# Layer one of a decoder trunk: VectorE turns three of a head's ten blocks of probabilities

## The chip, the cores and the metric

The kernel runs on one core of one Trainium2 chip. The metric is the device time of one execution in microseconds (us); less is better. All times below are of the kernel before the change.

## The reference, cut to what matters

The trunk has two layers over 512 tokens of width 1024, all in float32. Layer one is sparse attention: 16 heads of 128, one shared key and value, and for each query the 128 keys that an indexer has chosen. Layer two is a dilated window attention with 16 heads. Each layer ends in a gated output projection.

```python
s = jnp.einsum('bqhd,bqkd->bhqk', qb, k_sel).astype(jnp.float32)
s = jnp.where(valid[:, None], s, -jnp.inf)
p = jax.nn.softmax(s, axis=-1).astype(v.dtype)
return jnp.einsum('bhqk,bqkd->bqhd', p, v_sel)
...
return (o * jax.nn.silu(z)) @ w_out
```

The kernel does layer one's attention over all causal keys, with a bias that rules out those which were not chosen.

## The kernel before, in words

Every product of two float32 matrices is made of three matmuls: each operand is split into a high half (`_hi`, made by ScalarE) and a low half (`_lo`, what is left, made by GpSimd for weights and queries), and high by high, high by low and low by high are added in PSUM. The program of each engine is written out by hand, and semaphores join them. Each engine takes its instructions in the order written. The two layers' heads are numbered through: n = 0 to 15 in layer one, 16 to 31 in layer two.

The scores of a head are four row blocks of 128 queries; block i has i+1 blocks of 128 keys, so that there are ten blocks of 128 by 128. In layer one `head_a(hd)` is one step of a pipeline over the heads, on each engine:

- TensorE: the scores of head hd-2 (`scores`), half of the query projection of head hd (`project`, eight steps of three matmuls), the output of head hd-3 (`output`, for each block column j three matmuls, after a wait for the low half of that column), the other half of the projection, and then `turn_probs(hd - 2)`: the ten blocks of probabilities are turned with ten matmuls against the identity, into three PSUM banks (column 0 with four blocks, column 1 with three, columns 2 and 3 with three).
- VectorE: `mask_scores` (bias, negation and row maximum of the scores), `rope` of head hd-1's query (two products with the sine, one with the cosine, one sum), `invert` (the reciprocal of the four row sums), `gate` of head hd-3 (its output times the SiLU of the gate), `probs_lo` (the low halves of the turned probabilities, one instruction for each bank).
- ScalarE: the high half of a weight tile (`split_w`), `exps` (the four exponentials with their sums), the query's high half, `probs_hi` (the high halves of the turned probabilities, one for each bank).
- GpSimd: the low half of a weight tile (`split_w`), `normalise` (the four row blocks of probabilities times the inverse of their sums), the query's low half (`rope_lo`).

`head_a` runs for hd = 0 to 18, and heads 0 to 15 are attended in steps 2 to 17. In step 17 there is no rotation but a gate's scaling. After step 18 TensorE goes on to the output projection of layer one. Layer two turns nearly all its blocks on VectorE (`turn_blocks`): sixteen instructions, each of which turns the 32 by 32 parts of all ten blocks at one place (32 partitions, ten blocks of 32 elements).

Of the kernel before, what the change touches and what calls it, by code (L numbers as in the profile page):

```python
# [7 lines left out]
F32 = mybir.dt.float32  # L8
F32R = mybir.dt.float32r
ALU = mybir.AluOpType  # L10
ACT = mybir.ActivationFunctionType

P = 128
# [3 lines left out]
HEADS, HEAD_DIM = 16, 128  # L17
# [12 lines left out]
OFF = [P * i * (i + 1) // 2 for i in range(QB)]  # L30
COLS = P * QB * (QB + 1) // 2
T_OFF = [0, SEQ, SEQ + 3 * P, SEQ + 5 * P]
# [11 lines left out]
G_Q = [G_Z[-1] + 1] + list(range(G_Z[-1] + 3, G_Z[-1] + 2 + HEADS + LATE_GATES))  # L44
# [21 lines left out]
R_Q = R_K + 1  # L66
# [20 lines left out]
S_BANK, T_BANK = 2, 5  # L87
# [12 lines left out]
CUT = T_OFF[2]  # L100
# [3 lines left out]
def turned_before(n):  # L104

    by_vector = sum(x in VECTOR_HEADS for x in range(n))
    return n - by_vector, by_vector
# [7 lines left out]
def build(nc, xT, x_rows, gains, weights, rope_tables, dilated_bias, causal_bias, ident_in, outT, out_rows):  # L115
    with ExitStack() as ctx:
# [3 lines left out]
        def sem(name):  # L120
            return ctx.enter_context(nc.semaphore(name))

        ps = ctx.enter_context(nc.psum_tensor("ps", [P, 8, SEQ], F32))
# [35 lines left out]
        probs = sb("probs", [P, COLS])  # L159
# [3 lines left out]
        pT_hi = sb("pT_hi", [P, COLS], F32R)  # L163
        pT_lo = sb("pT_lo", [P, COLS], F32R)
# [12 lines left out]
        score = sb("score", [P, COLS - P])  # L177
        left = neg_s[:, 0:COLS - P]

        turned = bias_a  # L180

        ordered = neg_s
# [15 lines left out]
        inv_den = sb("inv_den", [P, QB])  # L198
# [38 lines left out]
            sem("scores_done"), sem("scores_read"), sem("exp_done"), sem("inv_ready"), sem("probs_ready"))  # L237
        blocks_turned, turned_hi_ready, turned_lo_ready = (
            sem("blocks_turned"), sem("turned_hi_ready"), sem("turned_lo_ready"))
        probs_turned, pT_hi_ready, pT_lo_ready, o_done, gated_ready = (  # L240
            sem("probs_turned"), sem("pT_hi_ready"), sem("pT_lo_ready"), sem("o_done"), sem("gated_ready"))
        o_lo_ready, o_hi_ready, y_done, residual_ready = (
# [88 lines left out]
        def _(pe):  # L331
# [141 lines left out]
            def turn_probs(n):  # L473
                pe.wait_ge(probs_ready, n * QB + QB)
                if n:
                    pe.wait_ge(gated_ready, n)
                for b, js in enumerate(((0,), (1,), (2, 3))):
                    for j in js:
                        for i in range(j, QB):
                            at = T_OFF[j] - T_OFF[js[0]] + (i - j) * P  # L480
                            src = OFF[i] + j * P
                            last = pe.transpose(ps[:, T_BANK + b, at:at + P], probs[:, src:src + P], ident[:, :])  # L482
                    last.then_inc(probs_turned, 1)
# [18 lines left out]

            def output(n, high, low):
                for j in range(QB):
                    pe.wait_ge(pT_lo_ready, turned_before(n)[0] * 3 + min(j, 2) + 1)
                    out = ps[:, T_BANK, j * P:SEQ]
                    vs, cols = slice(j * P, (j + 1) * P), slice(T_OFF[j], T_OFF[j] + SEQ - j * P)
                    pe.matmul(out, high[:, vs], pT_hi[:, cols], start=(j == 0), stop=False)
                    pe.matmul(out, high[:, vs], pT_lo[:, cols], start=False, stop=False)  # L509
                    last = pe.matmul(out, low[:, vs], pT_hi[:, cols], start=False, stop=(j == QB - 1))  # L510
                last.then_inc(o_done, 1)
# [209 lines left out]
        def _(act):  # L721
# [109 lines left out]
            def exps(n):  # L831
                by_tensor, by_vector = turned_before(n)
                if by_vector:

                    act.wait_ge(probs_ready, n * QB)
                elif by_tensor:
                    act.wait_ge(probs_turned, by_tensor * 3)
                for i in range(QB):
                    act.wait_ge(scores_read, n * QB + i + 1)
                    cols = slice(OFF[i], OFF[i] + (i + 1) * P)  # L840
                    act.activation(probs[:, cols], neg_s[:, cols], ACT.Exp, bias=neg_max[:, i:i + 1], scale=-1.0,  # L841
                                   accum_out=den[:, i:i + 1]).then_inc(exp_done, 1)

            def probs_hi(n):
                for b, (at, end) in enumerate(((0, T_OFF[1]), (T_OFF[1], T_OFF[2]), (T_OFF[2], COLS))):
                    act.wait_ge(probs_turned, turned_before(n)[0] * 3 + b + 1)
                    act.activation(pT_hi[:, at:end], ps[:, T_BANK + b, 0:end - at],  # L847
                                   ACT.Copy).then_inc(pT_hi_ready, 1)

            def turned_hi(n):  # L850
                act.wait_ge(blocks_turned, turned_before(n)[1] + 1)
# [159 lines left out]
        def _(dve):  # L1011
# [121 lines left out]
                dve.tensor_tensor(rotated[:, R_K % 2, :], by_cos[:, :], by_sin[:, :],  # L1133
                                  ALU.add).then_inc(rotated_ready, 1)

            def rope(r, g):
                n, half = n_of(g), P // 2

                past = r - R_IQ - 1 - (r > R_K) - (r > R_B)
                dve.wait_ge(tile_done, g + 1)  # L1140
                dve.wait_ge(*rotated_at(r - 1))
                for out, other in ((slice(0, half), slice(half, P)), (slice(half, P), slice(0, half))):
                    dve.tensor_tensor(by_sin[out, :], ps[other, BANK[n], :], scaled[other, 1, :],  # L1143
                                      ALU.mult).then_inc(sin_ready, 1)

                dve.wait_ge(sin_ready, 2 * past + 2)
                dve.tensor_tensor(ps[:, BANK[n], :], ps[:, BANK[n], :], scaled[:, 0, :], ALU.mult).then_inc(cos_ready, 1)
                dve.wait_ge(cos_ready, past + 1)
                dve.wait_ge(rope_lo_ready, r - 1)
                dve.tensor_tensor(rotated[:, r % 2, :], ps[:, BANK[n], :], by_sin[:, :],  # L1150
                                  ALU.add).then_inc(bank_read[BANK[n]], 1)
# [80 lines left out]
            def turn_blocks(n):  # L1232
# [9 lines left out]
                                             source[rows_at:rows_at + 32, :, cols_at:cols_at + 32])  # L1242
                last.then_inc(blocks_turned, 1)

            def probs_lo(n):
                for b, (at, end) in enumerate(((0, T_OFF[1]), (T_OFF[1], T_OFF[2]), (T_OFF[2], COLS))):
                    dve.wait_ge(pT_hi_ready, turned_before(n)[0] * 3 + b + 1)
                    dve.tensor_tensor(pT_lo[:, at:end], ps[:, T_BANK + b, 0:end - at],  # L1248
                                      pT_hi[:, at:end].bitcast(F32), ALU.subtract).then_inc(pT_lo_ready, 1)
# [31 lines left out]
            def head_a(hd):  # L1281
                attend, roped, finish = 2 <= hd < HEADS + 2, 1 <= hd < HEADS + 1, 3 <= hd < HEADS + 3
                if attend:
                    mask_scores(hd - 2, bias_a, lambda i: OFF[i])
                if roped:
                    rope(R_Q + hd - 1, G_Q[hd - 1])
                if attend:
                    invert(hd - 2)
                if hd > HEADS:
                    z = hd - LATE_GATES - 1  # L1290
                    scale_gate(z, G_Z[z])
                if finish:
                    gate(hd - 3, hd - 3)
                if attend:
                    probs_lo(hd - 2)

            def head_b(hd):
# [164 lines left out]
        def _(pool):  # L1462
# [42 lines left out]
            def normalise(n):  # L1505
                pool.wait_ge(inv_ready, n + 1)
                for i in (3, 2, 1, 0):
                    cols = slice(OFF[i], OFF[i] + (i + 1) * P)
                    pool.tensor_scalar(probs[:, cols], probs[:, cols], inv_den[:, i:i + 1], 1.0, ALU.mult,  # L1509
                                       ALU.mult).then_inc(probs_ready, 1)  # L1510

            def order(n):

                pool.wait_ge(inv_ready, n + 1)
                blocks = ordered[:, :].rearrange("p (b c) -> p b c", c=P)
                for i in (3, 2, 1, 0):
                    for first, count, place, step in GROUPS[i]:
                        cols = slice(OFF[i] + first * P, OFF[i] + (first + count) * P)
                        last = pool.tensor_scalar(blocks[:, place:place + (count - 1) * step + 1:step, :],  # L1519
                                                  probs[:, cols].rearrange("p (b c) -> p b c", c=P),  # L1520
                                                  inv_den[:, i:i + 1], 1.0, ALU.mult, ALU.mult)
                    last.then_inc(probs_ready, 1)

            def turned_lo(n):
                number = turned_before(n)[1]
                pool.wait_ge(o_done, n)
                for k, part in enumerate((slice(0, CUT), slice(CUT, COLS))):
                    pool.wait_ge(turned_hi_ready, 2 * number + k + 1)
                    pool.tensor_tensor(pT_lo[:, part], turned[:, part], pT_hi[:, part].bitcast(F32),  # L1529
                                       ALU.subtract).then_inc(turned_lo_ready, 1)  # L1530

            def head_a(hd):
                attend, rope = 2 <= hd < HEADS + 2, 1 <= hd < HEADS + 1
                if 0 < hd < HEADS + LATE_GATES:
                    split_w(G_Q[hd] + 2)
                if attend:
                    normalise(hd - 2)
                if rope:
                    slot = (hd - 1) % 2
                    rope_lo(R_Q + hd - 1, q_hi[:, slot, :], q_lo[:, slot, :])  # L1540
# [135 lines left out]
```

## Time and profile before

| what | value |
| --- | --- |
| median of 3 runs | 932.15 us (931.74 to 933.51) |
| the profiled execution | 931.12 us |
| its span in the profile | 929.3 us |
| busy share of the span: TensorE matmuls, VectorE, ScalarE, GpSimd | 99%, 65%, 46%, 59% |

The span is the part of the execution that the profiler saw; 1.8 us of the execution lie around it. A busy share is the mean over the whole span, in which stages with different limits follow on one another: the attention of layer one runs from about 163 to 329 us.

### The profile page before, as it was taken

The numbers are of one execution on the slowest core, as the hardware profiler recorded it, in microseconds if no ns is written. First come the engines' busy times: TensorE is split into PE (matmuls) and PEld (weight loads), VectorE is DVE, ScalarE is ACT, GpSimd is POOL, SyncE is SP. The second block draws the span as 40 slices with busy tenths as digits, with TensorE's granted clock in tenths as the row PEclk, the third lists the DMA queues.
The fourth block names the chain that finished last, engine by engine and source line by source line (L and its number), as shares of the span: only waits on it lengthen the run. The fifth ranks groups of instructions, "written<-read, shape, count | busy, mean of one in ns | idle before, by whom it ended". The sixth has DMA issues, their size and how long they took to land.

```text
span 929.3 us, 13299 instructions
## 1 busy us (share of the span) xinstructions
PE 920.9 (99%) x4865; PEld 801.1 (86%) x4865; DVE 600.5 (65%) x1283; ACT 426.5 (46%) x776; POOL 551.7 (59%) x419
## 2 busy tenths in 40 slices
PE   9999999999999999999999999999999999999997
PEld 8898888788888888889898898989898888988887
DVE  7898898676677541145776666667767666665234
ACT  6765333454455542253443535452443435453334
POOL 2776545555555544457666677666766667774544
PEclk9999999999999999999999999999999999999999
DMA  8322322112111122222222222222222222132412
GB/s 335 134 92 82 123 91 91 46 46 68 46 46 47 67 84 98 95 88 69 70 90 92 91 80 65 83 92 89 71 70 90 91 91 81 56 114 69 129 53 91
DMA packets 24689, 81.48 MB, mean 88 GB/s; under 512 B 2864, under 2 KB 4144, under 8 KB 24624
## 3 DMA queue, kind: packets, MB, share of 16 engines
q1 hardware_dynamic: 23472, 79.06, 25.7%
q10 hardware_dynamic: 1152, 1.57, 0.5%
q8 instruction: 39, 0.64, 0.3%
q14 instruction: 26, 0.21, 0.1%
HBM read 78.52 MB, written 2.10 MB: 87 GB/s over the span
## 4 chain that ended last, share of the span: by engine, by line
PE 95%; DVE 2%; POOL 1%; issue 0%; DMA 0%; ACT 0%; DVEq 0%; SPq 0%; POOLq 0%
PE ps L384 17%; PE ps L385 17%; PE ps L386 17%; PE ps L518 6%; PE ps L519 6%; PE ps L520 6%; PE ps L419 3%; PE ps L418 3%; PE ps L417 3%; PE ps L482 2%; PE ps L469 2%; PE ps L470 2%; PE ps L471 2%; PE ps L509 1%; PE ps L510 1%; PE ps L499 1%
## 5 line engine op out<-in xcount | busy, mean ns | idle before, releaser
L1468 POOL TENSOR_TENSOR w_lo<-w_raw,w_hi 128x1024 fp32r<-128x1024 f32 x136 | 329.4, 2429 | 175.0 <-ACT w_hi L726 174.3
L384 PE MATMUL ps<-u_hi,w_hi 128*128 128x512 f32 (+1 forms) x712 | 275.5, 387 | 0.3 <-POOL w_lo L1468 0.2
L385 PE MATMUL ps<-u_lo,w_hi 128*128 128x512 f32 (+1 forms) x712 | 274.5, 386 | 0.0
L386 PE MATMUL ps<-u_hi,w_lo 128*128 128x512 f32 (+1 forms) x712 | 274.5, 385 | 0.0
L384 PEld LDWEIGHTS ps<-u_hi,w_hi 128*128 128x128 f32 x712 | 133.7, 188 | 26.4 <-DVE u_lo L1057 0.6
L386 PEld LDWEIGHTS ps<-u_hi,w_lo 128*128 128x128 f32 x712 | 133.7, 188 | 25.8
L385 PEld LDWEIGHTS ps<-u_lo,w_hi 128*128 128x128 f32 x712 | 133.7, 188 | 25.3
L726 ACT ACTIVATE w_hi<-w_raw 128x1024 fp32r<-128x1024 f32 x136 | 141.7, 1053 | 25.7 <-DMA w_raw<-weights 16.4
L1241 DVE STREAM_TRANSPOSE bias_a<-neg_s 32x320 f32<-32x320 f32 x240 | 120.6, 503 | 25.1 <-POOL neg_s L1519 22.1
L841 ACT ACTIVATE probs<-neg_s,neg_max 128x128 f32<-128x128 f32 (+3 forms) x128 | 70.5, 552 | 51.9 <-DVE neg_max L1223 51.8
L1529 POOL TENSOR_TENSOR pT_lo<-bias_a,pT_hi 128x896 fp32r<-128x896 f32 (+1 forms) x30 | 46.6, 1574 | 70.4 <-ACT pT_hi L855 70.4
L855 ACT ACTIVATE pT_hi<-bias_a 128x896 fp32r<-128x896 f32 (+1 forms) x30 | 20.5, 731 | 126.9 <-DVE bias_a L1241 126.9
L419 PE MATMUL ps<-w_hi,u_lo 128*128 128x256 f32 x256 | 72.4, 283 | 0.0
L418 PE MATMUL ps<-w_lo,u_hi 128*128 128x256 f32 x256 | 72.4, 283 | 0.0
L417 PE MATMUL ps<-w_hi,u_hi 128*128 128x256 f32 x256 | 72.4, 283 | 0.0
L1519 POOL TENSOR_SCALAR neg_s<-probs,inv_den 128x256 f32<-128x256 f32 x90 | 38.9, 453 | 54.0 <-DVE inv_den L1230 54.0
L1143 DVE TENSOR_TENSOR by_sin<-ps,scaled 64x512 f32<-64x512 f32 x94 | 64.7, 689 | 4.7 <-PE ps L386 0.7
L1248 DVE TENSOR_TENSOR pT_lo<-ps,pT_hi 128x384 fp32r<-128x384 f32 (+1 forms) x51 | 27.5, 596 | 53.9 <-ACT pT_hi L847 53.9
L1509 POOL TENSOR_SCALAR probs<-probs,inv_den 128x512 f32<-128x512 f32 (+1 forms) x68 | 35.4, 541 | 39.7 <-DVE inv_den L1230 39.7
L518 PE MATMUL ps<-o_hi,w_hi 128*128 128x512 f32 (+1 forms) x136 | 51.6, 379 | 0.0
L519 PE MATMUL ps<-o_lo,w_hi 128*128 128x512 f32 (+1 forms) x136 | 51.2, 377 | 0.0
L520 PE MATMUL ps<-o_hi,w_lo 128*128 128x512 f32 (+1 forms) x136 | 51.2, 377 | 0.0
(206 smaller groups left out, 1729.3 us busy)
## 6 DMA issues: line engine op xcount, KB each, us to landing
w_raw<-weights SPq DMA_DIRECT2D x136, 512.0 KB, 3.3
gated<-x_rows SPq DMA_DIRECT2D x4, 512.0 KB, 8.0
h<-x_turned SPq DMA_DIRECT2D x7, 256.0 KB, 5.6
w_raw<-weights SPq DMA_DIRECT2D x4, 256.0 KB, 4.7
table<-rope_tables SPq DMA_DIRECT2D x2, 512.0 KB, 7.2
neg_s<-weights SPq DMA_DIRECT2D x1, 512.0 KB, 6.8
outT<-h ACTq DMA_DIRECT2D x4, 128.0 KB, 1.7
outT<-h SPq DMA_DIRECT2D x4, 128.0 KB, 1.9
```

The costliest lines, as they stand in the source:

```text
L384: pe.matmul(out, w_hi[:, g % SLOTS, blk], u_hi[:, k, tokens], start=(at == 0), stop=False)
L385: pe.matmul(out, w_hi[:, g % SLOTS, blk], u_lo[:, k, tokens], start=False, stop=False)
L386: last = pe.matmul(out, w_lo[:, g % SLOTS, blk], u_hi[:, k, tokens], start=False, stop=(at == KT - 1))
L417: pe.matmul(out, u_hi[:, k, tokens], high, start=(j % 2 == 0 and at == 0), stop=False)
L418: pe.matmul(out, u_hi[:, k, tokens], low, start=False, stop=False)
L419: last = pe.matmul(out, u_lo[:, k, tokens], high, start=False, stop=(j % 2 == 1 and at == KT - 1))
L518: pe.matmul(out, w_hi[:, g % SLOTS, blk], hi[:, tokens], start=first, stop=False)
L519: pe.matmul(out, w_hi[:, g % SLOTS, blk], lo[:, tokens], start=False, stop=False)
L520: return pe.matmul(out, w_lo[:, g % SLOTS, blk], hi[:, tokens], start=False, stop=final)
L726: act.activation(w_hi[:, g % SLOTS, :], w_raw[:, g % 2, :], ACT.Copy).then_inc(w_hi_ready, 1)
L1241: last = dve.transpose(target[cols_at:cols_at + 32, :, rows_at:rows_at + 32], source[rows_at:rows_at + 32, :, cols_at:cols_at + 32])
L1468: pool.tensor_tensor(w_lo[:, g % SLOTS, :], w_raw[:, g % 2, :], w_hi[:, g % SLOTS, :].bitcast(F32), ALU.subtract).then_inc(w_lo_ready, 1)
```

## The change

For the heads of layer one alone:

- TensorE turns seven blocks (columns 0 and 1) and no longer the last three (column 2's two and column 3's one).
- GpSimd (`normalise_apart` in place of `normalise`) writes these three blocks, normalised, to the space `apart` first, and then the other seven in place: six instructions in place of four.
- VectorE turns the three blocks from `apart` to `apart_turned` in sixteen instructions (`turn_apart`, 32 partitions and three blocks of 32 elements each), after `gate` and ahead of `probs_lo`, which makes two low halves in place of three.
- ScalarE makes the high half of the third part from `apart_turned` in place of a PSUM bank, and so waits for VectorE there.
- GpSimd makes the third part's low half (`apart_lo`), as the first instruction of the next step.
- TensorE's `output` waits for that low half ahead of column 2.
- VectorE's `invert` moves from behind the rotation to between the rotation's two products with the sine and the one with the cosine.

```diff
+        apart, apart_turned = score[:, 0:3 * P], score[:, 3 * P:6 * P]
...
-                for b, js in enumerate(((0,), (1,), (2, 3))):
+                for b, js in enumerate(((0,), (1,)) if n < HEADS else ((0,), (1,), (2, 3))):
...
-                    pe.wait_ge(pT_lo_ready, turned_before(n)[0] * 3 + min(j, 2) + 1)
+                    if n < HEADS and j == 2:
+                        pe.wait_ge(apart_lo_ready, n + 1)
+                    elif j < 3:
+                        pe.wait_ge(pT_lo_ready, 2 * turned_before(n)[0] + j + 1)
...
+                    if n < HEADS and b == 2:
+                        act.wait_ge(apart_done, n + 1)
+                        source = apart_turned
+                    else:
+                        act.wait_ge(probs_turned, 2 * turned_before(n)[0] + b + 1)
+                        source = ps[:, T_BANK + b, 0:end - at]
+                    act.activation(pT_hi[:, at:end], source, ACT.Copy).then_inc(pT_hi_ready, 1)
...
+                if inverted is not None:
+                    invert(inverted)
...
+            def turn_apart(n):
+                dve.wait_ge(apart_ready, n + 1)
+                if n:
+
+                    dve.wait_ge(pT_hi_ready, 3 * n)
+                    dve.wait_ge(apart_lo_ready, n)
+                source, target = (t.rearrange("p (b c) -> p b c", c=P) for t in (apart, apart_turned))
+                for rows_at in range(0, P, 32):
+                    for cols_at in range(0, P, 32):
+                        last = dve.transpose(target[cols_at:cols_at + 32, :, rows_at:rows_at + 32],
+                                             source[rows_at:rows_at + 32, :, cols_at:cols_at + 32])
+                last.then_inc(apart_done, 1)
...
                 if roped:
-                    rope(R_Q + hd - 1, G_Q[hd - 1])
-                if attend:
+                    rope(R_Q + hd - 1, G_Q[hd - 1], hd - 2 if attend else None)
+                elif attend:
                     invert(hd - 2)
...
                 if attend:
+                    turn_apart(hd - 2)
                     probs_lo(hd - 2)
...
+            def normalise_apart(n):
+
+                pool.wait_ge(inv_ready, n + 1)
+                if n:
+                    pool.wait_ge(apart_done, n)
+                for i, at in ((3, P), (2, 0)):
+                    cols = slice(OFF[i] + 2 * P, OFF[i] + (i + 1) * P)
+                    last = pool.tensor_scalar(apart[:, at:at + (i - 1) * P], probs[:, cols], inv_den[:, i:i + 1], 1.0,
+                                              ALU.mult, ALU.mult)
+                last.then_inc(apart_ready, 1)
+                for i in (3, 2, 1, 0):
+                    cols = slice(OFF[i], OFF[i] + min(i + 1, 2) * P)
+                    pool.tensor_scalar(probs[:, cols], probs[:, cols], inv_den[:, i:i + 1], 1.0, ALU.mult,
+                                       ALU.mult).then_inc(probs_ready, 1)
...
+            def apart_lo(n):
+                pool.wait_ge(pT_hi_ready, 3 * n + 3)
+                pool.tensor_tensor(pT_lo[:, CUT:COLS], apart_turned, pT_hi[:, CUT:COLS].bitcast(F32),
+                                   ALU.subtract).then_inc(apart_lo_ready, 1)
...
+                if hd >= 3:
+                    apart_lo(hd - 3)
                 if 0 < hd < HEADS + LATE_GATES:
                     split_w(G_Q[hd] + 2)
                 if attend:
-                    normalise(hd - 2)
+                    normalise_apart(hd - 2)
```

On VectorE, a step of layer one from the rotation to the next head's scores stands in this order in the kernel before (out<-in, partitions by elements):

```order
L1143 TENSOR_TENSOR by_sin<-ps,scaled 64x512 x2
L1147 TENSOR_TENSOR ps<-ps,scaled 128x512
L1150 TENSOR_TENSOR rotated<-ps,by_sin 128x512
L1230 RECIPROCAL inv_den<-den 128x4
L1273 TENSOR_TENSOR gated<-ps,gated 128x512
L1248 TENSOR_TENSOR pT_lo<-ps,pT_hi 128x512
L1248 TENSOR_TENSOR pT_lo<-ps,pT_hi 128x384 x2
L1220 TENSOR_TENSOR neg_s<-ps,bias_a 128x128
```

In the changed kernel the same place, after the two products with the sine and the moved reciprocal, reads:

```order
L1161 TENSOR_TENSOR ps<-ps,scaled 128x512
L1164 TENSOR_TENSOR rotated<-ps,by_sin 128x512
L1302 TENSOR_TENSOR gated<-ps,gated 128x512
L1268 STREAM_TRANSPOSE score<-score 32x3x32 x16
L1277 TENSOR_TENSOR pT_lo<-ps,pT_hi 128x512
L1277 TENSOR_TENSOR pT_lo<-ps,pT_hi 128x384
L1234 TENSOR_TENSOR neg_s<-ps,bias_a 128x128
```

Sixteen turning instructions have come between `gate` and the low halves, one low half of 384 columns has gone, and the next head's scores stand behind all of them.

On GpSimd, a step in the kernel before, from the weight tile's low half on:

```order
L1468 TENSOR_TENSOR w_lo<-w_raw,w_hi 128x1024
L1509 TENSOR_SCALAR probs<-probs,inv_den 128x512
L1509 TENSOR_SCALAR probs<-probs,inv_den 128x384
L1509 TENSOR_SCALAR probs<-probs,inv_den 128x256
L1509 TENSOR_SCALAR probs<-probs,inv_den 128x128
L1492 TENSOR_TENSOR q_lo<-rotated,q_hi 128x512
```

And in the changed kernel:

```order
L1550 TENSOR_SCALAR score<-probs,inv_den 128x256
L1550 TENSOR_SCALAR score<-probs,inv_den 128x128
L1555 TENSOR_SCALAR probs<-probs,inv_den 128x256 x3
L1555 TENSOR_SCALAR probs<-probs,inv_den 128x128
L1523 TENSOR_TENSOR q_lo<-rotated,q_hi 128x512
L1580 TENSOR_TENSOR pT_lo<-score,pT_hi 128x384
L1499 TENSOR_TENSOR w_lo<-w_raw,w_hi 128x1024
```

The normalising has six instructions, the three blocks for VectorE first, and the third part's low half stands between the query's low half and the next weight tile's.

## Rows read from the trace of the kernel before

**Rows 1.** The page's first part: busy time, share of the span, instructions.

```profile
PE 920.9 (99%) x4865; PEld 801.1 (86%) x4865; DVE 600.5 (65%) x1283; ACT 426.5 (46%) x776; POOL 551.7 (59%) x419
```

**Rows 2.** Busy time by engine in one step's window: PE, PEld, DVE, ACT, POOL, granted clock.

```profile
239.41:249.72 10.31, 10.31 (x59) 9.03 (x57) 7.00 (x19) 5.26 (x15) 5.71 (x6) 1.00 0.15 53
```

**Rows 3.** Timeline of VectorE, one step: start, us, what, idle before.

```profile
308.65 0.28 DVE L1220 TENSOR_TENSOR neg_s<-ps,bias_a 128x128 f32<-128x128 f32 x1
...
310.74 1.41 DVE L1143 TENSOR_TENSOR by_sin<-ps,scaled 64x512 f32<-64x512 f32 x2
...
313.52 0.17 DVE L1230 RECIPROCAL inv_den<-den 128x4 f32<-128x4 f32 x1
313.60 0.66 DVE L1273 TENSOR_TENSOR gated<-ps,gated 128x512 f32<-128x512 f32 x1
317.42 1.62 DVE L1248 TENSOR_TENSOR pT_lo<-ps,pT_hi 128x512 fp32r<-128x512 f32 x3 [3.16 <-ACT pT_hi L847]
318.96 0.28 DVE L1220 TENSOR_TENSOR neg_s<-ps,bias_a 128x128 f32<-128x128 f32 x1
```

**Rows 4.** Timeline of TensorE: the turning, and what comes next.

```profile
316.16 1.25 PE L482 MATMUL ps<-ident,probs 128*128 128x128 f32 x10
317.17 0.36 PE L462 MATMUL ps<-k_both,q_hi 128*128 128x256 f32 x1
```

**Rows 5.** Layer two's turning on VectorE: its line's view, then its timeline.

```profile
L1241 DVE STREAM_TRANSPOSE bias_a<-neg_s x240: 498/503/509, 447.5 to 817.8; 32x320 f32<-32x320 f32 x120
499.18 1.53 DVE L1241 STREAM_TRANSPOSE bias_a<-neg_s 32x320 f32<-32x320 f32 x3 [0.47 <-POOL neg_s L1519]
```

**Rows 6.** VectorE by line and shape, 180 to 290 us: busy us, mean ns, idle before.

```profile
L1223 DVE CUSTOM_DVE_ANT_0 neg_s<-ps,bias_a 128x512 f32<-128x512 f32 x11 | 7.5, 686 | 0.0
...
L1223 DVE CUSTOM_DVE_ANT_0 neg_s<-ps,bias_a 128x256 f32<-128x256 f32 x11 | 4.6, 421 | 0.0
...
L1220 DVE TENSOR_TENSOR neg_s<-ps,bias_a 128x128 f32<-128x128 f32 x11 | 3.1, 282 | 0.0
L1230 DVE RECIPROCAL inv_den<-den 128x4 f32<-128x4 f32 x10 | 1.7, 169 | 0.0
```

**Rows 7.** GpSimd by line and shape, 445 to 810 us.

```profile
L1519 POOL TENSOR_SCALAR neg_s<-probs,inv_den 128x256 f32<-128x256 f32 x60 | 28.0, 478 | 54.0 <-DVE inv_den L1230 54.0
...
L1529 POOL TENSOR_TENSOR pT_lo<-bias_a,pT_hi 128x384 fp32r<-128x384 f32 x14 | 14.3, 1023 | 0.0
L1519 POOL TENSOR_SCALAR neg_s<-probs,inv_den 128x128 f32<-128x128 f32 x30 | 12.1, 403 | 0.0
```

**Rows 8.** Timelines of ScalarE and GpSimd in a step, and of GpSimd in layer two.

```profile
310.86 0.71 ACT L841 ACTIVATE probs<-neg_s,neg_max 128x512 f32<-128x512 f32 x1
315.81 1.28 POOL L1492 TENSOR_TENSOR q_lo<-rotated,q_hi 128x512 fp32r<-128x512 f32 x1
319.18 2.42 POOL L1468 TENSOR_TENSOR w_lo<-w_raw,w_hi 128x1024 fp32r<-128x1024 f32 x1 [2.09 <-ACT w_hi L726]
...
499.11 4.75 POOL L1468 TENSOR_TENSOR w_lo<-w_raw,w_hi 128x1024 fp32r<-128x1024 f32 x2
```

**Rows 9.** Timeline of VectorE, the first attended head.

```profile
168.43 0.17 DVE L1230 RECIPROCAL inv_den<-den 128x4 f32<-128x4 f32 x1
173.25 1.62 DVE L1248 TENSOR_TENSOR pT_lo<-ps,pT_hi 128x512 fp32r<-128x512 f32 x3 [4.66 <-ACT pT_hi L847]
174.78 0.28 DVE L1220 TENSOR_TENSOR neg_s<-ps,bias_a 128x128 f32<-128x128 f32 x1
```

**Rows 10.** Timelines of VectorE, ScalarE and TensorE, the last attended head.

```profile
324.01 0.69 DVE L1273 TENSOR_TENSOR gated<-ps,gated 128x512 f32<-128x512 f32 x1 [1.24 <-ACT gated L829]
325.72 1.36 ACT L847 ACTIVATE pT_hi<-ps 128x512 fp32r<-128x512 f32 x3 [1.81 <-PE ps L482]
327.57 0.39 PE L508 MATMUL ps<-pT_hi,v_hi 128*128 128x512 f32 x1
...
328.77 0.29 PE L508 MATMUL ps<-pT_hi,v_hi 128*128 128x256 f32 x1
```

More of the change, by code:

```diff
@@ L239, in build @@
             sem("blocks_turned"), sem("turned_hi_ready"), sem("turned_lo_ready"))
+        apart_ready, apart_done, apart_lo_ready = sem("apart_ready"), sem("apart_done"), sem("apart_lo_ready")
         probs_turned, pT_hi_ready, pT_lo_ready, o_done, gated_ready = (
@@ L836, in exps @@
                 elif by_tensor:
-                    act.wait_ge(probs_turned, by_tensor * 3)
+                    act.wait_ge(probs_turned, 2 * by_tensor)
                 for i in range(QB):
@@ L845, in probs_hi @@
                 for b, (at, end) in enumerate(((0, T_OFF[1]), (T_OFF[1], T_OFF[2]), (T_OFF[2], COLS))):
-                    act.wait_ge(probs_turned, turned_before(n)[0] * 3 + b + 1)
-                    act.activation(pT_hi[:, at:end], ps[:, T_BANK + b, 0:end - at],
-                                   ACT.Copy).then_inc(pT_hi_ready, 1)
+                    if n < HEADS and b == 2:
[5 more added lines that the diff above has]
+                    act.activation(pT_hi[:, at:end], source, ACT.Copy).then_inc(pT_hi_ready, 1)
             def turned_hi(n):
@@ L1134, in key_rope, with rope @@
                                   ALU.add).then_inc(rotated_ready, 1)
-            def rope(r, g):
+            def rope(r, g, inverted=None):
                 n, half = n_of(g), P // 2
@@ L1243, in turn_blocks @@
                 last.then_inc(blocks_turned, 1)
+            def turn_apart(n):
[9 more added lines that the diff above has]
+                last.then_inc(apart_done, 1)
             def probs_lo(n):
-                for b, (at, end) in enumerate(((0, T_OFF[1]), (T_OFF[1], T_OFF[2]), (T_OFF[2], COLS))):
+                parts = ((0, T_OFF[1]), (T_OFF[1], T_OFF[2]), (T_OFF[2], COLS))
+                for b, (at, end) in enumerate(parts[0:2] if n < HEADS else parts):
                     dve.wait_ge(pT_hi_ready, turned_before(n)[0] * 3 + b + 1)
```

## The prediction

> **What bounds the kernel now.** The page comes first: TensorE has matmuls in flight for 99% of the span, and the busiest other engine, VectorE, works for 65% of it [rows 1]. The busy time in the window of one step of layer one then shows this stage's own limit: TensorE is busy for all of its 10.31 us, at the full granted clock (1.00), VectorE for 7.00 and GpSimd for 5.71 [rows 2]. So a step lasts as long as TensorE's work in it, and what the others have to spare is room. VectorE's timeline shows how large the room is and where it lies: from one head's first mask instruction (308.65) to the next one's (318.96) pass 10.31 us, and the only large gap is the 3.16 us ahead of the low halves [rows 3]. All else on VectorE takes 10.31 - 3.16 = 7.15 us.
>
> **What TensorE saves.** The ten turns take 317.17 - 316.16 = 1.01 us until the next matmul starts, 0.101 each [rows 4]. Three fewer give 0.30 us for a head and 4.85 us for 16 heads. TensorE would then need 10.01 us for a step. That is all the change can give, and VectorE has to keep up with 10.01 for it.
>
> **What VectorE takes on.** No instruction of the trace turns 96 elements, so the price of the sixteen has to be bounded. The same operation with 320 elements takes 503 ns, and three of them in a row take 1.53 us, so that one starts (1.53 - 0.503) / 2 = 0.514 us after the other: 11 ns more than it lasts, with no overlap [rows 5]. How it scales is the question on which all depends:
> - In proportion to the elements it would be 0.3 of 0.514, 0.154 us. I exclude this: a reciprocal of four elements alone lasts 169 ns [rows 6].
> - With that instruction as floor, and the 11 ns: 0.18 us. This is the lower bound.
> - VectorE's other work grows by (686 - 421) / 256 = 1.035 ns an element [rows 6]. Taken off the 503 ns for 224 fewer elements, 271 ns are left, with the 11 ns 0.282 us. This is nearest in kind, and I take it.
> - The nearest row in size, 128 columns in 282 ns [rows 6], less 32 elements at that slope and with the 11 ns gives 0.26 us.
> - With no gain from the smaller size: 0.514 us, the upper bound.
>
> Call this pitch p. The sixteen take 16p - 0.01 us. Out of VectorE's step goes the third low half: three take 1.54 us from 317.42 to 318.96 [rows 3], and of the 384 wide one I take 0.46. Two new waits on other engines, ahead of the turning and behind it, cost about 0.03 each. The moved reciprocal costs the same in its new place. VectorE's step becomes 7.15 - 0.46 + 0.06 - 0.01 + 16p = 6.74 + 16p. At p = 0.282 that is **11.25 us**, more than TensorE's 10.01 and more than the 10.31 of before: VectorE becomes the bound and a head costs 0.94 us more. TensorE's step is shorter than VectorE's from p = 0.204 on, and above p = 0.223 the change loses in every step.
>
> The Trainium skill speaks to this price ("VectorE: DVE Perf Modes"). Its section on the TRN2 errata has VectorE's SBUF instructions cost 58 cycles and one for each element at 0.96 GHz, by which 320 elements would take 394 ns. The trace has 503 for them, so it does not agree. By the rule a turn of 96 would be 160 ns, and an estimate by it is a step of 9.3 us on VectorE, so that TensorE would stay the bound. The section on the three transpose paths gives 311 ns for VectorE on 128 by 128 in bf16; no run here shows that one, and as an estimate it would put 96 elements near 0.28 us.
>
> **Do the others fit into 11.25 us?** I follow one step from T, the end of the sixteen turns.
> - ScalarE's third high half: three take 1.36 us [rows 10], so about 0.5, done at T+0.5; GpSimd's third low half 1.02 us [rows 7], done at T+1.6; the weight tile's low half 2.42 [rows 8], done at T+4.1.
> - VectorE makes its two low halves (1.1) and starts the mask at T+1.1. From the mask's start the two products with the sine end after 312.15 - 308.65 = 3.5 us [rows 3], and the last exponential is done earlier, after 2.9 [rows 8]. So the inverse comes at T+4.7, when GpSimd is free.
> - GpSimd's six instructions cost four times 0.478 and two times 0.403 [rows 7], 2.7 us: `apart` is ready at T+5.6, all probabilities at T+7.5, the query's low half at T+8.8 (1.28 more).
> - VectorE has ended `gate` at T+1.1 + 5.6 = T+6.7 (314.26 - 308.65 before [rows 3]), later than `apart` is ready. This is what the moved inverse does: in its old place, 1.3 us later, VectorE would stand for some 0.2 us here.
> - TensorE turns seven blocks at T+7.5, begins the scores at T+8.8 and has them done by T+10.7; VectorE masks them at T+12.4. Its output's wait for the third low half (T+12.9 in the next round) comes behind half a projection and is over before it is reached (T+13.4).
>
> So nothing makes the step longer than VectorE's own work. TensorE loses 11.25 - 10.01 = 1.2 us a step, ahead of the turning (for GpSimd's probabilities) and ahead of the scores (for the query's low half).
>
> **The sum.** Head 0 has more room, since TensorE's step is longer there: VectorE ends the rotation about 168.6, the turns 173.1, two low halves 174.3, against 174.78 before [rows 9]: -0.5 us. The next fourteen masks follow 11.25 apart in place of 10.31: +13.2. The last attended head has no rotation, so here TensorE's wait is the limit. From its mask's start M (318.96 before), `gate` ends at M+5.7 (324.70 [rows 10]), the turns at M+10.3, the first low half at M+11.0, the second at M+11.5, GpSimd's third at M+11.9. Output column 0 starts at M+11.0 and column 2 1.2 us later at M+12.2, in place of 328.77 = M+9.8 [rows 10]: +2.4. Behind it TensorE has the output projection and layer two, in which it works without a gap of note [rows 1], so the delay stays. Sum: -0.5 + 13.2 + 2.4 = **+15.1 us**. On the profiled execution's 931.12 this gives 946.2, and since that lies 1.03 under the median of 932.15, the median comes to 947.3; I say 947.
>
> **The rivals.**
> - *VectorE becomes the bound* (my forecast). For it: the 503 ns and the slope in its own engine's rows. At p = 0.26 (step 10.90) the sum is -0.8 + 8.3 + 2.1 = 9.6, at p = 0.30 (step 11.54) -0.2 + 17.2 + 2.7 = 19.7: 941 to 953. 0.80.
> - *TensorE stays the bound; faster.* It needs p below 0.204, a fixed part near the reciprocal's 169 ns and little else, or a fixed part that the next instruction hides as it does between the mask's instructions. Against it: the turns of 320 do not overlap at all [rows 5]. The gain is 4.85 less up to 1 us at the last head: 928. This is where the skill's 58 cycles would lead. 0.11. At p from 0.204 to 0.223 the two effects cancel and the time is within 0.2%: 0.03.
> - *VectorE waits as well.* If GpSimd is slower while VectorE turns (against it: beside layer two's turning, from 499.18 on, two weight tiles' low halves take 4.75 us, as fast as layer one's 2.42 each [rows 5, 8]), or if the inverse reaches it late, the turning starts late: 0.5 us a step give 15 x 0.5 = 7.5 more, 954 to 955. 0.06 together with the upper bound p = 0.514, whose step of 15.0 us would give about 1,000.
>
> **How the numbers follow.** The likeliest case and the lower part of the last give slower with 0.86; faster 0.11; same 0.03. A change under 0.2% (1.9 us) could not be told from none. The likeliest case holds 941 to 953 with 0.80 less its own tails. To hold 8 in 10 the range takes in a pitch down to about 0.24 (a step of 10.6, +5 us) and half of the waiting case: 936 to 955.
>
> **What would show it.** Right: in the changed profile VectorE is busy for 95% or more of a step of layer one, the step is about 11.2 us between masks, a turn takes near 270 ns, TensorE has gaps of some 0.7 and 0.5 us ahead of the turning and of the scores, and layer two's steps are as before. Wrong: a turn of under 0.2 us with steps of 10.0; or turns as priced, but a longer step with idle time on VectorE ahead of the turning. The weakest number is the turn's fixed part, since sixteen of it lie in each step: 10 ns in it move the result by 2.4 us.

## The result and the profile after

The changed kernel takes 947.49 us (median of 6 runs, 946.59 to 947.93), the kernel before 932.50 (6 runs on the same chip): a ratio of 1.016, with a 95% interval of 1.0147 to 1.0173. The forecast was 947, slower, with a range of 936 to 955.

The page of the changed kernel, its first part (to be held against [rows 1]):

```profile
PE 924.5 (98%) x4817; PEld 796.2 (84%) x4817; DVE 663.0 (70%) x1523; ACT 428.5 (45%) x776; POOL 575.0 (61%) x467
```

TensorE has 48 instructions fewer, VectorE 240 more and 62 us more of work. The averages show no bound on VectorE, since 70% is far from full. The step does. Two steps of layer one in windows that reach from one head's first mask instruction to the next one's (to be held against [rows 2]):

```profile
309.22:320.35 11.13, 10.44 (x55) 8.64 (x54) 10.74 (x34) 5.39 (x14) 7.16 (x10) 1.00 0.16 48
320.35:331.49 11.14, 10.45 (x55) 8.64 (x54) 10.75 (x35) 5.40 (x14) 7.17 (x10) 1.00 0.15 49
```

The window is 11.13 us where it was 10.31. TensorE's busy time no longer fills it, and VectorE's 10.74 does but for the small gaps between its instructions. VectorE's timeline of that step (to be held against [rows 3]):

```profile
309.22 0.28 DVE L1234 TENSOR_TENSOR neg_s<-ps,bias_a 128x128 f32<-128x128 f32 x1
...
311.30 1.41 DVE L1155 TENSOR_TENSOR by_sin<-ps,scaled 64x512 f32<-64x512 f32 x2
312.74 0.18 DVE L1244 RECIPROCAL inv_den<-den 128x4 f32<-128x4 f32 x1
312.83 0.67 DVE L1161 TENSOR_TENSOR ps<-ps,scaled 128x512 f32<-128x512 f32 x1
313.54 0.69 DVE L1164 TENSOR_TENSOR rotated<-ps,by_sin 128x512 f32<-128x512 f32 x1
314.15 0.68 DVE L1302 TENSOR_TENSOR gated<-ps,gated 128x512 f32<-128x512 f32 x1
314.75 4.50 DVE L1268 STREAM_TRANSPOSE score<-score 32x96 f32<-32x96 f32 x16
319.28 1.16 DVE L1277 TENSOR_TENSOR pT_lo<-ps,pT_hi 128x512 fp32r<-128x512 f32 x2
320.35 0.28 DVE L1234 TENSOR_TENSOR neg_s<-ps,bias_a 128x128 f32<-128x128 f32 x1
```

No row has an idle time behind it in brackets: the 3.16 us ahead of the low halves are gone. The turning takes 4.50 us in one piece. The waits are now on TensorE, in the timeline of the same step (to be held against [rows 4]):

```profile
315.60 0.98 PE L487 MATMUL ps<-ident,probs 128*128 128x128 f32 x7 [0.44 <-POOL probs L1555]
316.84 0.39 PE L466 MATMUL ps<-k_both,q_hi 128*128 128x256 f32 x1 [0.25 <-POOL q_lo L1523]
```

They stand at the two places named beforehand, ahead of the turning (for the normalised probabilities) and ahead of the scores (for the query's low half). The brackets count from the end of the matmul before. By the starts, the turning comes 0.60 us and the scores 0.56 us later than they would right behind the matmuls before them, where 0.7 and 0.5 were forecast. Together that is what TensorE loses in a step: 11.13 us, against 9.96 in a kernel in which it doesn't wait (half of the turns, below). The chain that ended last shows VectorE's part over the whole program; before, 95% of it lay on TensorE and 2% on VectorE:

```profile
PE 76%; DVE 17%; issue 3%; DMA 2%; ACT 1%; POOL 1%; SPq 0%; DVEq 0%; ACTq 0%; POOLq 0%
```

**Where the time went.** The mask instructions of the heads are marks that both traces have. From mask 0 to the end of the span it is 765.75 us before (163.55 to 929.3) and 780.87 after (164.83 to 945.7): 15.12 more.

| stretch | before | after | difference | forecast |
| --- | --- | --- | --- | --- |
| mask 0 to mask 1 | 11.23 | 10.77 | -0.46 | -0.5 |
| mask 1 to mask 15 | 144.18 | 155.89 | +11.71 | +13.2 |
| mask 15 to layer two's first mask | 122.65 | 126.51 | +3.86 | +2.4 |
| from there to the end | 487.69 | 487.70 | +0.01 | 0 |

Mask 0 itself stands 1.28 us later after (164.83 for 163.55), ahead of all that was changed. In the other profiles of this study it stands at 164.35 or later, so this is taken for a difference between executions; the medians lie 15.0 us apart.

### The profile page after: what moved, and what is told of

The parts are those of the page before. It is cut to its first block, busy times and chain, and to the rows that moved or that the text cites. A ratio compares the mean times of both kernels' runs of the same rounds, so it can differ in the third digit from the quotient of the medians.

```text
span 945.7 us, 13521 instructions
## 1 busy us (share of the span) xinstructions
PE 924.5 (98%) x4817; PEld 796.2 (84%) x4817; DVE 663.0 (70%) x1523; ACT 428.5 (45%) x776; POOL 575.0 (61%) x467
## 4 chain that ended last, share of the span: by engine, by line
PE 76%; DVE 17%; issue 3%; DMA 2%; ACT 1%; POOL 1%; SPq 0%; DVEq 0%; ACTq 0%; POOLq 0%
PE ps L388 13%; PE ps L389 13%; PE ps L390 13%; DVE score L1268 6%; PE ps L526 6%; PE ps L528 6%; PE ps L527 6%; PE ps L423 3%; PE ps L422 3%; PE ps L421 3%; DVE by_sin L1155 2%; DVE pT_lo L1277 2%; DMA gated<-x_rows 1%; DVE u_lo L1069 1%; DVE neg_s L1237 1%
## 5 line engine op out<-in xcount | busy, mean ns | idle before, releaser
L1268 DVE STREAM_TRANSPOSE score<-score 32x96 f32<-32x96 f32 x256 | 68.8, 269 | 3.2
L1302 DVE TENSOR_TENSOR gated<-ps,gated 128x512 f32<-128x512 f32 x32 | 22.0, 686 | 44.1 <-PE ps L505 39.7
```

The lines of the kernel that those rows point to most:

```text
L1268: last = dve.transpose(target[cols_at:cols_at + 32, :, rows_at:rows_at + 32], source[rows_at:rows_at + 32, :, cols_at:cols_at + 32])
```

## The experiments

Theory A in all of them: VectorE's own queue, with sixteen turns of nearly fixed price, sets the step of the changed kernel. Its rivals are named with each. The first four ran on one chip, beside 932.03 us for the kernel before; the next four on a second, beside 932.31; the last two on a third, beside 932.07. Each ratio is to the kernel before on the same chip. A difference between two other kernels can be one between chips, on which the kernel before differs by up to 0.5 us.

**Half of the turns.** Is it VectorE's length, or the longer chain through ScalarE and GpSimd?

```diff
+                if n == 0:
+                    dve.memset(target[:, :, P // 2:P], 0.0)
-                for rows_at in range(0, P, 32):
+                for rows_at in range(0, P // 2, 32):
```

> The changed kernel with eight of the sixteen turning instructions left out (half of the rows of the three blocks are not turned, a zero stands there), all waits kept. Theory A (the length of VectorE's queue is the bound, sixteen times 0.282 us of it the turning): VectorE's step falls to 11.13 - 8 x 0.282 = 8.9 us, TensorE is the bound again with its three turns saved: steps of 10.0 us and 927.5 to 928.5 us in all, under the kernel before. Theory B (the longer chain through ScalarE and GpSimd is the bound, and VectorE only happens to be busy): steps stay over 10.3 us, 932 us or more.

Measured: 926.75 us (4 runs, 926.71 to 926.87), ratio 0.994 (0.9924 to 0.9957). The window of one step:

```profile
244.40:254.36 9.96, 9.96 (x56) 8.68 (x54) 8.67 (x26) 5.28 (x14) 7.21 (x10) 1.00 0.15 53
```

TensorE fills it again, and VectorE needs 8.67. All waits and the whole detour over ScalarE and GpSimd are still there; only eight instructions of a head are gone. So the detour costs nothing by itself, and TensorE's saving is real as soon as VectorE has the room. It is a little larger than forecast, as TensorE's timeline of this kernel shows:

```profile
252.02 0.93 PE L487 MATMUL ps<-ident,probs 128*128 128x128 f32 x7
252.70 0.36 PE L466 MATMUL ps<-k_both,q_hi 128*128 128x256 f32 x1
```

Seven turns take 0.68 us until the next matmul, where ten took 1.01 [rows 4]: 0.33 saved, not 0.30. The result lies 0.75 us under the expected range. Two causes can be seen: this 0.03 us in each step, and the interval from mask 1 to mask 2, which is 8.87 us where the kernel before has 10.10 (the moved inverse, see below).

**Narrower turns.** Is the price of a turn fixed, or does it go with the elements? The third block of each turn is left out:

```diff
-                        last = dve.transpose(target[cols_at:cols_at + 32, :, rows_at:rows_at + 32],
-                                             source[rows_at:rows_at + 32, :, cols_at:cols_at + 32])
+                        last = dve.transpose(target[cols_at:cols_at + 32, 0:2, rows_at:rows_at + 32],
+                                             source[rows_at:rows_at + 32, 0:2, cols_at:cols_at + 32])
```

> The changed kernel with each of the sixteen turning instructions over two of the three blocks (64 elements; the third block is not turned). Theory A (a large fixed part, 1.04 ns an element on top): an instruction every 0.249 us, 0.53 us less a step, steps of 10.6 us, 939 to 940 us in all. Theory B (the price goes with the elements): an instruction every 0.188 us, VectorE's step 9.6 us, TensorE the bound at 10.0, 930 us or less.

Measured: 938.24 us (4 runs, 937.83 to 940.12), ratio 1.0067 (1.0052 to 1.0082): theory A, though 0.8 us under the expected range. VectorE's timeline:

```profile
244.49 3.96 DVE L1268 STREAM_TRANSPOSE score<-score 32x64 f32<-32x64 f32 x16
248.48 1.16 DVE L1277 TENSOR_TENSOR pT_lo<-ps,pT_hi 128x512 fp32r<-128x512 f32 x2
249.56 0.28 DVE L1234 TENSOR_TENSOR neg_s<-ps,bias_a 128x128 f32<-128x128 f32 x1
...
260.16 0.28 DVE L1234 TENSOR_TENSOR neg_s<-ps,bias_a 128x128 f32<-128x128 f32 x1
```

A third less to turn takes the sixteen from 4.50 to 3.96 us, and the step to 260.16 - 249.56 = 10.60, as expected. What is missing to 939 lies in the last head: from mask 15 to the end of the span it is 612.6 us here and 614.2 in the changed kernel (see the last head by TensorE). Together with the line's view of this kernel and of the changed one the price is known at three widths, the third from [rows 5]:

```profile
L1268 DVE STREAM_TRANSPOSE score<-score x256: 222/236/243, 169.5 to 333.2; 32x64 f32<-32x64 f32 x128
```

```profile
L1268 DVE STREAM_TRANSPOSE score<-score x256: 253/269/276, 169.8 to 341.4; 32x96 f32<-32x96 f32 x128
```

From 64 to 96 elements it is 33 ns for 32, from 96 to 320 it is 234 ns for 224: 1.03 and 1.04 ns an element, on a fixed part of some 169 ns.

**The inverse back in its old place.**

```diff
-                    rope(R_Q + hd - 1, G_Q[hd - 1], hd - 2 if attend else None)
-                elif attend:
+                    rope(R_Q + hd - 1, G_Q[hd - 1])
+                if attend:
                     invert(hd - 2)
```

> The changed kernel with the inverse of the sums back behind the rotation. Theory A (VectorE's own queue sets the step, and the moved inverse keeps it free of waits): the inverse comes 1.3 us later, the three blocks apart are ready about 0.4 us after the gate ends, so each of 14 to 15 turnings starts 0.4 to 0.5 us later: 953 to 955 us, with that wait on GpSimd seen ahead of the turning. Theory B (GpSimd is ready early enough in either place): 947.5 us, no wait.

Measured: 954.87 us (4 runs, 953.64 to 955.23), ratio 1.0239 (1.0224 to 1.0254): theory A, 7.4 us more than the changed kernel. Its masks lie 11.62 us apart in place of 11.13. In its timeline VectorE waits once in each step:

```profile
250.68 0.66 DVE L1302 TENSOR_TENSOR gated<-ps,gated 128x512 f32<-128x512 f32 x1
251.72 4.52 DVE L1268 STREAM_TRANSPOSE score<-score 32x96 f32<-32x96 f32 x16 [0.39 <-POOL score L1550]
```

From the gate's start to the turning's it is 1.04 us in place of 0.60. So the moved inverse is what keeps GpSimd's three blocks ahead of VectorE.

**The last head by TensorE.** What does the end of layer one cost? The change is bound to a set of heads, here 0 to 14, and each counter of the semaphores is counted over that set:

```diff
+APART = range(HEADS - 1)
...
-                for b, js in enumerate(((0,), (1,)) if n < HEADS else ((0,), (1,), (2, 3))):
+                for b, js in enumerate(((0,), (1,)) if n in APART else ((0,), (1,), (2, 3))):
```

> The changed kernel, but the last head of layer one (head 15) has all ten blocks turned by TensorE as before. Theory A (the end of layer one costs 3.7 us of the loss, of which about 1.5 us are matmuls at half the clock after TensorE's wait of 2.7 us): 943.4 us, no wait over 1 us ahead of the last output and no matmuls at half clock there. Theory B (the end costs the 2.4 us that I had priced and the rest lies elsewhere): 945 us.

Measured: 943.40 us (4 runs, 943.09 to 944.47), ratio 1.012 (1.0105 to 1.0136): theory A; 4.1 us lie in the last head. The traces say so too, by what follows mask 15: 614.2 us in the changed kernel, 610.2 here. What they are made of shows in TensorE's timeline of the changed kernel at that place (to be held against [rows 10]):

```profile
337.38 0.98 PE L487 MATMUL ps<-ident,probs 128*128 128x128 f32 x7 [1.31 <-POOL probs L1555]
...
342.42 0.79 PE L516 MATMUL ps<-pT_hi,v_hi 128*128 128x512 f32 x1 [2.67 <-DVE pT_lo L1277]
343.01 0.63 PE L517 MATMUL ps<-pT_lo,v_hi 128*128 128x512 f32 x1
...
344.82 0.41 PE L516 MATMUL ps<-pT_hi,v_hi 128*128 128x256 f32 x1
...
345.80 0.44 PE L526 MATMUL ps<-o_hi,w_hi 128*128 128x512 f32 x1
```

and in two windows of it:

```profile
342.40:345.80 3.40, 3.38 (x13) 3.10 (x13) 2.04 (x3) 1.65 (x4) 0.89 (x1) 0.53 0.00 0
345.80:356.00 10.20, 10.20 (x47) 8.46 (x47) 7.08 (x5) 4.34 (x6) 5.14 (x3) 1.00 0.15 51
```

TensorE waits 1.31 us, turns, works a little and waits 2.67 us for the low halves (a wait that the kernel before doesn't have). Then a matmul of 512 columns lasts 0.63 us in place of 0.39, and the granted clock of the stretch is 0.53: nearly all of it at the lower level of 1.2 GHz. Head 15's output takes 345.80 - 342.42 = 3.38 us; head 14's, at the full clock, took 1.85 (332.63 to 334.48). That is 1.5 us, and in the stretch behind the clock is back at 1.00. In the kernel of this experiment TensorE waits once there, 1.28 us ahead of the turning (for the gate), and its matmuls of 512 columns stay at 0.39. The kernel with narrower turns waits 0.79 and then 2.11 us at this place; its granted clock stays at 1.00, and from the start of head 15's output to the output projection it takes 2.2 us in place of 3.4. This is why it came out under its range.

**The inverse alone, on the kernel before.**

```diff
+                if inverted is not None:
+                    invert(inverted)
...
-                    rope(R_Q + hd - 1, G_Q[hd - 1])
-                if attend:
+                    rope(R_Q + hd - 1, G_Q[hd - 1], hd - 2 if attend else None)
+                elif attend:
                     invert(hd - 2)
```

> The kernel before with one part of the change alone: the inverse of the sums between the sine and the cosine products. Theory A (TensorE is the bound of a step and never waits for GpSimd there): no difference, 931.5 to 932.5 us; GpSimd's normalising starts 1.2 us earlier in a step, unused. Theory B (the inverse's place is worth something by itself): faster by 0.2% or more.

Measured: 930.52 us (11 runs, 929.60 to 930.96), ratio 0.9979 (0.9970 to 0.9988). Here I was wrong: it is faster by 1.8 us, 0.21% with an interval of 0.12% to 0.30%, which is theory B's side. The timeline of TensorE in the kernel before and then in this one, at the turning of head 1, has the cause:

```profile
182.03 1.31 PE L482 MATMUL ps<-ident,probs 128*128 128x128 f32 x10 [1.64 <-POOL probs L1509]
```

```profile
181.50 1.31 PE L482 MATMUL ps<-ident,probs 128*128 128x128 f32 x10 [0.31 <-POOL probs L1511]
```

Three of the eight steps of the query projection that belongs into this step of the pipeline were already done in the step before, so TensorE's step is short there and it does wait for GpSimd, 1.64 us before and 0.31 now. From mask 0 to mask 15 it is 153.94 us in place of 155.41; where the other 0.3 us of the 1.8 lie is not shown. This wait comes once, and I had looked at windows of later heads.

**Every other head.** A turning head leaves VectorE 11.13 - 10.01 = 1.1 us behind TensorE. Does a head without it make up for that? The heads that turn are 0, 2, ... 14.

```diff
+APART = range(0, HEADS - 1, 2)
```

> The changed kernel with the change in heads 0, 2, 4, ... 14 alone; the other heads have all ten blocks turned by TensorE. Theory A (a turning step leaves VectorE 1.1 us behind TensorE; the moved inverse gives GpSimd 1.2 us of room, so that the next head's query and probabilities are still in time, and VectorE catches up in that step): no waits on TensorE, each of the 8 heads saves its 0.30 us, 2.4 us in all: 929.2 to 930.2 us, faster than the kernel before. Theory B (TensorE waits in each step in which VectorE is late): 932 us or more.

Measured: 929.37 us (6 runs, 928.95 to 930.53), ratio 0.9968 (0.9957 to 0.9980): faster than the kernel before. The windows of a turning head and of the next one:

```profile
285.52:296.66 11.14, 11.14 (x61) 9.65 (x60) 10.74 (x34) 5.12 (x14) 6.69 (x9) 1.00 0.15 49
296.66:305.77 9.11, 9.11 (x53) 8.05 (x53) 6.99 (x20) 5.51 (x14) 6.24 (x7) 1.00 0.19 58
```

The masks are 11.14 and 9.11 us apart, 20.25 for two heads where 20.60 were needed, and TensorE is busy in all of it: VectorE is late for one head and on time for the next.

The time is in the expected range, but not all by the expected way. That range took 2.4 us for the turns alone, and "no waits". The moved inverse is in this kernel too, and alone it gave 930.52 us on the same chip. So the turning by itself is worth 1.15 us by the medians, and the ranges of the two kernels overlap. In the traces it shows: from mask 0 to mask 15 it is 152.38 us, and 153.94 with the inverse alone. Two waits of TensorE are left, 0.17 us at head 1's turning and 0.78 at head 15's.

**Two of three heads.**

```diff
+APART = [n for n in range(HEADS - 1) if n % 3 < 2]
```

> As the kernel with every other head, but with the change in heads 0, 1, 3, 4, 6, 7, ... 13 (ten heads). Theory A (the room is between 1.1 and 1.5 us, and two turning steps in a row put VectorE 2.2 us behind): about 0.8 us of waits in each group of three heads, against 0.6 saved: 932 to 934 us. Theory B (the room holds two in a row): ten heads save 3.0 us, 929 us.

Measured: 933.66 us (10 runs, 932.71 to 934.72), ratio 1.0014 (1.0005 to 1.0023): theory A. A group takes 11.31 + 11.13 + 8.77 = 31.21 us between masks, where three heads at TensorE's pace would take 30.3: 0.9 us lost in each group, 0.8 expected.

**Every other head, inverse back.** The set of every other head with the diff of the inverse's old place.

> As the kernel with every other head, with the inverse back behind the rotation. Theory A (the moved inverse is what gives the room): a turning step is late by 1.5 us, the room is 0.3 us or none, so about 1.4 us of waits for each pair of heads: 936 to 941 us. Theory B (the room lies elsewhere): 930 us, as with the inverse moved.

Measured: 941.68 us (4 runs, 940.22 to 941.76), ratio 1.0094 (1.0081 to 1.0108). The way is theory A's, and the size is 0.7 us beyond its range: 12.3 us more than with the inverse moved. The masks place it. From mask 4 on a pair of heads takes 21.73 us, 1.48 more than the 20.25 with the inverse moved (1.4 expected). The first two pairs take 2.9 and 1.7 more. There TensorE waits 2.35 us at head 1's turning, and its ten turns behind that take 2.39 us in place of 1.31, at a granted clock of 0.63 and then 0.52, which the expectation didn't have.

**Without head 14, and every other head again.** The larger of the two waits that are left with every other head stands in TensorE's timeline at head 15's turning:

```profile
322.79 1.28 PE L500 MATMUL ps<-ident,probs 128*128 128x128 f32 x10 [0.78 <-DVE gated L1316]
```

```diff
-APART = range(0, HEADS - 1, 2)
+APART = range(0, HEADS - 2, 2)
```

> As the kernel with every other head, but head 14 is left to TensorE: the change in heads 0, 2, ... 12 alone. In the trace of the kernel with every other head TensorE waits 0.78 us for a gate ahead of head 15's turning, since VectorE is late from head 14. Theory A (that wait comes from head 14's turning): it is gone, at the price of one saving of 0.30 us: 0.5 us faster than with head 14, 928.9 us, which the times alone can hardly show and the trace can. Theory B (the wait belongs to the end of the layer as such): 0.3 us slower, 929.7 us, with the wait still there.

> The kernel with every other head once more, beside the one without head 14: 929.4 us, with the 0.78 us wait ahead of head 15's turning, and about 3 us faster than the kernel before.

Measured: 928.77 us (6 runs, 928.33 to 930.20; ratio 0.9966, 0.9954 to 0.9978) without head 14, 929.66 (7 runs, 929.05 to 930.20; ratio 0.9974, 0.9963 to 0.9985) with it. TensorE's waits in layer one are 0.8 us for the gate and 0.2 for probabilities in the second, and there is none in the first, so theory A holds by the trace; the times overlap and don't tell the two apart. The version with seven heads is the fastest of those that still compute the reference, 3.3 us under the kernel before. Of these, 1.8 are the moved inverse's. The seven heads' turning adds 1.5 by the medians (on another chip) and 2.4 by the spans of the profiled executions (926.3 us, and 928.7 with the inverse alone), which is seven times the 0.33 us of a head. Part of the difference lies outside the span, where the kernel with seven heads has 2.3 us in place of 1.8; the cause of that is open.

## Why the prediction was right, point by point

- **TensorE saves 0.30 us a head and VectorE has to keep up.** Right in kind; with half the turns the step is 9.96 us and the whole 926.75. The saving is 0.33: the forecast took a tenth of the ten turns' time for each, and three fewer save a little more than that. In the changed kernel this term is not seen, since VectorE sets the step.
- **A turn every 0.282 us.** Right: sixteen take 4.50 us, (4.50 - 0.269) / 15 = 0.282. It was taken from the 503 ns at 320 elements and the slope of VectorE's other work; the price in proportion (0.154) is refuted by the narrower turns, which save 0.034 us each and not a third, and the floor from the reciprocal (0.18) was far too low: even 64 elements take 0.236. The Trainium skill's 58 cycles and one for each element ("VectorE: DVE Perf Modes", the TRN2 errata) would make an estimated 160 ns of 96 elements, and the trace has 269. The prediction left out that the same section of the Trainium skill says of this row that it under-predicts, and puts the measured fixed term at about 150 cycles. With that term an estimate for 96 elements is 256 ns and for 320 it is 490. The traces have 269 and 503, 13 ns more for both, and so agree with this term and not with the 58 cycles.
- **VectorE's step of 11.25 us.** It is 11.13. The term that was too large is the gate's end with the wait behind it: from the gate's start to the first turn pass 0.60 us, where I had counted 0.66 and 0.03, which is 0.09 of the 0.12. The sixteen turns (4.50) and the wait between them and the low halves (0.03) are as forecast. Fourteen steps came to 11.7 us more in place of 13.2.
- **Nothing makes the step longer than VectorE's work.** Right, as VectorE has no idle time in brackets in its step. The place of the inverse was under-priced: without the move I had 0.2 us of waiting, the experiment has 0.39 in brackets and 7.4 us in all.
- **The last head, +2.4.** It is 3.86 in the trace and 4.1 in the experiment. The late low halves were foreseen (output from M+11.0; it is M+10.9) and the consequence wasn't: 1.5 us of it are matmuls at the lower clock behind a wait of 2.67 us. The prediction has no term for the clock.
- The two misses, -1.5 and +1.5, cancel. That the forecast of 947 meets 947.49 so closely is luck; the parts are right to about 1.5 us each.
- **The rivals.** TensorE as the bound needed a turn under 0.204 us; it is 0.282. The extra wait of 0.5 us a step, for which VectorE would have had to stand ahead of the turning, was not there; it comes when the inverse is put back. Its other cause, a GpSimd that slows down beside VectorE's turning, is not there either: the query's low half, which runs beside the turns, lasts 1.27 us, and 1.28 in the kernel before [rows 8].
- **"The moved reciprocal costs the same", read as worth nothing to the kernel before.** On VectorE it costs the same (2.85 us from the first sine product to the gate, 2.86 before). To the kernel before it is worth 1.8 us, at head 1 above all. In the changed kernel that gain is buried, since VectorE sets that step too. In all kernels that turn in some heads only it is part of the time, so those have to be held against 930.5 as much as against the kernel before.

## What to carry to other kernels

Room on an engine is read in the step, not on the page: 65% busy left VectorE 3.2 us a head, and an exchange of 0.30 us on the bound engine for 4.0 on another had to be held against just that. A piece of work that many small instructions make is priced by their count, and a row of the same operation at another size is the best source, with the slope of the engine's other rows. Where a step overdraws the room by less than the buffering between engines holds, doing it in every other step can keep the gain: here all sixteen heads lose 15 us, and with seven the kernel is 3.3 us faster. A change in several parts has to be taken apart before its gain is given to one of them: 1.8 of those 3.3 us come from one reciprocal moved a few instructions ahead.

## What the runs showed of the hardware

- VectorE's transposing of float32 on 32 partitions lasts 236, 269 and 503 ns for 64, 96 and 320 elements: 169 ns and 1.04 ns an element. The next one starts 13 ns after the end of the one before, where two of the mask's instructions in a row overlap by some 0.08 us.
- In the changed kernel TensorE's granted clock fell to 0.53 for the 3.4 us behind a wait of 2.67 us that followed one of 1.31, and was at 1.00 in the stretch behind. The clock fell in two other kernels too. With the inverse back it did so at head 15 as well, about 1.3 us after the end of a wait of 2.66 us that followed one of 0.47 (0.50 from 351.5 to 353.0 us). With every other head and the inverse back it fell at a wait of 2.35 us at head 1 (0.52 from 185 to 187 us).
- It stayed at 1.00, or the matmuls of 512 columns at 0.39 us, behind waits of 0.79 and then 2.11 us (narrower turns), a single one of 1.28 (last head by TensorE), one of 1.64 (the kernel before, head 1), and 0.44 and 0.25 in each step of the changed kernel.
